# Summing a paged cache's four pieces per sample by accumulating gathers, three samples in turn, instead of by VectorE additions

## The reference, cut to what matters

```python
s16 = kv_cmp.reshape(B, n16, CMP_STRIDE, 2, KVH_D, HD_D).sum(axis=2)
cmp = (s16[:, :-1] + s16[:, 1:]) / CMP_BLOCK
kc = rms_norm(cmp[:, :, 0], kc_gain)
vc = cmp[:, :, 1]
```

## Time and profile before

| | |
|---|---|
| median of 3 runs | 1304.25 us (1300.81 to 1307.91) |
| the profiled execution, its own time | 1298.92 us |
| its span (first to last instruction) | 1297.1 us, so 1.8 us lie around it |
| mean granted TensorE clock | 0.979 |
| busy in the span: PE, DVE, POOL, ACT | 94%, 43%, 39%, 34% |

### The profile page before, as it was taken

One profiled execution on the slowest core, in us unless ns is written; L12 is line 12 of the kernel. 1 busy time (PEld: TensorE's weight loads), 2 busy tenths in 40 slices (PEclk: granted clock), 3 DMA queues, 4 the chain that ended last, 5 costly groups with the idle time before them and its releaser, 6 DMA issues.

```text
span 1297.1 us, 24311 instructions
## 1 busy us (share of the span) xinstructions
PE 1213.3 (94%) x10336; PEld 1137.1 (88%) x10336; DVE 557.2 (43%) x893; ACT 441.1 (34%) x713; POOL 503.7 (39%) x262
## 2 busy tenths in 40 slices
PE   7999979989999888899999878999999999999998
PEld 7998969988888877678887657999999999999998
DVE  4247643472337766664566554544322000222001
ACT  5432221124362223355444333333434211333111
POOL 3374441263135563322222451444343434344340
PEclk9999989889999999899999999999999999999999
DMA  5410101642136464311113493322222222222222
GB/s 202 148 65 34 66 33 58 140 127 66 51 99 212 163 210 131 130 57 58 65 51 129 159 337 116 139 98 83 97 84 94 87 93 98 81 97 81 99 81 82
DMA packets 47688, 139.52 MB, mean 108 GB/s; under 512 B 4470, under 2 KB 16090, under 8 KB 47210
## 3 DMA queue, kind: packets, MB, share of 16 engines
q1 hardware_dynamic: 37234, 100.50, 23.2%
q0 software_dynamic: 10368, 37.75, 8.5%
HBM read 129.98 MB, written 8.49 MB: 107 GB/s over the span
## 4 chain that ended last, share of the span: by engine, by line
PE 78%; DVE 13%; DMA 3%; issue 2%; ACT 2%; POOL 2%; SPq 0%; DVEq 0%; ACTq 0%
PE PS L614 46%; PE PS L847 11%; PE PS L659 7%; PE PS L715 2%; DVE M L1798 2%; PE PS L982 1%; DMA M<-cache_slc_kv,idx 1%; PE PS L1011 1%; PE PS L995 1%; DVE M L1801 1%; DMA M<-cache_cmp_kv,idx 1%; DVE xT L1662 1%; PE PS L810 1%; POOL WL L2198 1%; DVE M L1702 1%
## 5 line engine op out<-in xcount | busy, mean ns | idle before, releaser
L2198 POOL TENSOR_TENSOR WL<-M,WH 128x1024 fp32r<-128x1024 f32 x159 | 389.0, 2450 | 694.0 <-ACT WH L1189 693.7
L1189 ACT CAST WH<-M 128x1024 fp32r<-128x1024 f32 x159 | 165.8, 1046 | 266.3 <-DMA M<-weights 266.2
L614 PE MATMUL PS<-hH,WH 128*128 128x260 f32 x1040 | 215.5, 289 | 4.7 <-DVE M L1630 3.6
L614 PE MATMUL PS<-hH,WL 128*128 128x260 f32 x1040 | 212.7, 287 | 0.0
L614 PE MATMUL PS<-hL,WH 128*128 128x260 f32 x1040 | 212.3, 286 | 0.0
L614 PEld LDWEIGHTS PS<-hH,WH 128*128 128x128 f32 x1040 | 164.3, 193 | 8.2 <-issue 7.8
L614 PEld LDWEIGHTS PS<-hL,WH 128*128 128x128 f32 x1040 | 163.6, 192 | 0.0
L614 PEld LDWEIGHTS PS<-hH,WL 128*128 128x128 f32 x1040 | 163.5, 192 | 0.0
L847 PE MATMUL PS<-hH,WH 128*128 128x260 f32 x384 | 113.3, 295 | 4.5 <-ACT tmp L1345 2.9
L847 PE MATMUL PS<-hL,WH 128*128 128x260 f32 x384 | 109.7, 286 | 0.0
L847 PE MATMUL PS<-hH,WL 128*128 128x260 f32 x384 | 109.4, 285 | 0.0
(11 more groups left out here) (383 smaller groups left out, 2220.4 us busy)
## 6 DMA issues: line engine op xcount, KB each, us to landing
M<-weights SPq DMA_DIRECT2D x159, 512.0 KB, 3.3
M<-cache_win_kv POOLq DMA_DIRECT2D x7, 512.0 KB, 5.2
spill<-xT SPq DMA_DIRECT2D x1, 2080.0 KB, 8.7
M<-spill SPq DMA_DIRECT2D x1, 2080.0 KB, 7.8
M<-x_prompt SPq DMA_DIRECT2D x4, 512.0 KB, 5.4
con<-tables SPq DMA_DIRECT2D x1, 1437.5 KB, 12.5
M<-state_gla SPq DMA_DIRECT2D x2, 512.0 KB, 6.5
M<-state_hgrn SPq DMA_DIRECT2D x2, 512.0 KB, 11.0
```

Of the source, the lines that this page charges most:

```text
L614: last = mm(PS[:, bank + h, 0:HALF], w[:, slot_of(n), k, :], x[:, HALF * h:HALF * h + HALF], start=(start and k == k0 and w is WH and x is ...
L1189: nc.scalar.copy(WH[:, at].rearrange("p k n -> p (k n)"), WR[:, at]).then_inc(sem("w_hi"), 1)
L2198: p.tensor_tensor(WL[:, at].rearrange("p k n -> p (k n)"), WR[:, at], WH[:, at].rearrange("p k n -> p (k n)"), ALU.subtract).then_inc(sem( ...
```

## The change

The pieces of a sample are no longer brought to three slots in turn and added by DVE. A sample has one slot: its first piece is gathered into it, and the other three are gathered with an addition (`compute_op=ALU.add`), so that the DMA adds what it reads from the cache to what stands in the slot. A piece may be gathered only when the one before it in that slot has landed, so POOL waits for that slot's semaphore (`xc0` to `xc2`) ahead of each accumulating gather. Three samples go in turn, each in a slot of its own: samples 0 to 2, then 3 to 5, then 6 and 7 (numbered in the order in which they are taken). There are 32 gathers as before.

DVE is left with one L1798-like addition (512 columns) and the fold to 256 per sample. A table says at which step: C_GATHER for POOL, C_FOLD for DVE, C_PRODUCT for PE, C_COPY for DVE's copies out of bank 5. The third running sum takes the space of the former partial sum. The cache pieces after the stage wait for 8 in place of 32 counts of `c_free`.

```diff
-        CPIECES = [(x, c) for x in CSAMPLES for c in range(4)]
-        CSUM, CPART = [zt[:, 4, T:T + 512], zk[:, 1536:2048]], zk[:, 512:1024]
+        C_GATHER = {k: (n, c) for a, b, at in ((0, 3, -1), (3, 6, 15), (6, 8, 30)) for c in range(4)
+                    for n in range(a, b) for k in [at + 3 * c + n - a]}
+        C_FOLD = {12: 0, 13: 1, 14: 2, 28: 3, 29: 4, 30: 5, 42: 6, 43: 7}
+        C_PRODUCT = {15: (0, 1), 18: (2,), 31: (3,), 34: (4, 5), 45: (6, 7)}
+        C_COPY = {16: 0, 32: 2, 35: 4, 46: 6}
+        CSUM = [zt[:, 4, T:T + 512], zk[:, 1536:2048], zk[:, 512:1024]]
...
-                if k % 6 == 2 and 8 <= k <= 50:
-                    compressed_sum((k - 8) // 6)
+                for c in C_PRODUCT.get(k, ()):
+                    compressed_sum(c)
...
-                if k % 3 == 1 and k < 48:
-                    for q in (2 * (k // 3), 2 * (k // 3) + 1):
-                        n, c = q // 4, q % 4
-                        total = CSUM[n % 2]
-                        w = CRING[q % 3]
-                        dve.wait_ge(sem(f"xc{q % 3}"), 16 * (q // 3 + 1))
-                        if c == 0 and n >= 2:
-                            dve.wait_ge(sem("c_mm"), n - 1)
-                        v.tensor_tensor(CPART if c else total, w[:, 0:512], w[:, 512:1024], ALU.add).then_inc(sem("c_free"), 1)
-                        dve.wait_ge(sem("c_free"), q + 1)
-                        if c:
-                            step(v.tensor_tensor(total, total, CPART, ALU.add))
-                        if c == 3:
-                            v.tensor_tensor(total[:, 0:256], total[:, 0:256], total[:, 256:512], ALU.add)\
-                                .then_inc(sem("c_fold"), 1)
+                if k in C_FOLD:
+                    n = C_FOLD[k]
+                    w, total = CRING[n % 3], CSUM[n % 3]
+                    dve.wait_ge(sem(f"xc{n % 3}"), 64 * (n // 3 + 1))
+                    if n >= 3:
+                        dve.wait_ge(sem("c_mm"), n - 2)
+                    v.tensor_tensor(total, w[:, 0:512], w[:, 512:1024], ALU.add).then_inc(sem("c_free"), 1)
+                    dve.wait_ge(sem("c_free"), n + 1)
+                    v.tensor_tensor(total[:, 0:256], total[:, 0:256], total[:, 256:512], ALU.add)\
+                        .then_inc(sem("c_fold"), 1)
...
+            def compressed_gather(n, c):
+
+                if n >= 3 and c == 0:
+                    gp.wait_ge(sem("c_free"), n - 2)
+                if c:
+                    gp.wait_ge(sem(f"xc{n % 3}"), 16 * (4 * (n // 3) + c))
+                at = NI + NS * c + CSAMPLES[n]
+                src, row = rows("cache_cmp_kv"), bass.IndirectOffsetOnAxis(idx[:, at:at + 1], 0)
+                if c:
+                    gp.indirect_dma_start(CRING[n % 3], None, src, row, compute_op=ALU.add).then_inc(sem(f"xc{n % 3}"), 16)
+                else:
+                    gp.indirect_dma_start(CRING[n % 3], None, src, row).then_inc(sem(f"xc{n % 3}"), 16)
```

More of the change, by code:

```diff
@@ L858, in compressed_sum @@
                     pe.wait_ge(sem("sh_ev"), n // 2)
-                mm(PS[0:NCMP, 5, 256 * (x % 2):256 * (x % 2) + 256], C("shift", 0, NCMP), CSUM[n % 2][:, 0:256],
+                mm(PS[0:NCMP, 5, 256 * (x % 2):256 * (x % 2) + 256], C("shift", 0, NCMP), CSUM[n % 3][:, 0:256],
                    start=True, stop=True).then_inc(sem("c_mm"), 1)
@@ L1789, in mix_step @@
                             .then_inc(sem("mix_add"), 1)
[L1790 to L1806 removed]
+                if k in C_FOLD:
[8 more added lines that the diff above has]
+                        .then_inc(sem("c_fold"), 1)
+                if k in C_COPY:
+                    n = C_COPY[k]
                     x = CSAMPLES[n]
@@ L2262, in _ @@
             rows = lambda name: A[name].rearrange("o n (r t) a k d -> (o n r) (t a k d)", t=4)
-            def compressed_gather(q):
-                if q >= 3:
-                    gp.wait_ge(sem("c_free"), q - 2)
-                x, c = CPIECES[q]
-                gp.indirect_dma_start(CRING[q % 3], None, rows("cache_cmp_kv"),
-                                      bass.IndirectOffsetOnAxis(idx[:, NI + NS * c + x:NI + NS * c + x + 1], 0))\
-                  .then_inc(sem(f"xc{q % 3}"), 16)
+            def compressed_gather(n, c):
[9 more added lines that the diff above has]
+                    gp.indirect_dma_start(CRING[n % 3], None, src, row).then_inc(sem(f"xc{n % 3}"), 16)
             def mix_step(k):
@@ L2278, in mix_step @@
                     lower(N_MIX + 12 * bi + 3 * m + 1 + (s + 1) // 2)
-                if k % 3 == 2 and k < 47:
-                    for q in (2 * (k // 3) + 3, 2 * (k // 3) + 4):
-                        if q < len(CPIECES):
-                            compressed_gather(q)
+                if k >= 2 and k in C_GATHER:
+                    compressed_gather(*C_GATHER[k])
             def cache_piece(n):
@@ L2288, in cache_piece @@
                 if n == 0:
-                    gp.wait_ge(sem("c_free"), len(CPIECES))
+                    gp.wait_ge(sem("c_free"), NS)
                 if n == 2:
@@ L2310, in _ @@
             gp.wait_ge(sem("prod"), units_to_free(N_MIX - 4))
-            compressed_gather(0)
-            compressed_gather(1)
-            compressed_gather(2)
+            for n in range(3):
+                compressed_gather(n, 0)
             lower(N_MIX)
```

2 lines of the change are left out of this document (removed).

## The result

| | before | after |
|---|---|---|
| median of 9 runs | 1307.23 us | 1292.12 us |
| lowest and highest | 1300.76, 1314.66 | 1290.76, 1300.18 |
| the profiled execution | 1298.92 us | 1290.87 us |
| its mean granted clock | 0.979 | 0.979 |

The ratio after to before is 0.990, with a 95% interval of 0.9873 to 0.9927: 13 us faster. The forecast was 1288 us and a ratio of 0.9875. Between the two profiled executions the difference is 8.05 us where the forecast had 16.4. So two things have to be explained: why the traces show half of what was forecast, and why the medians show more than the traces. One further execution of the kernel before, among those timed beside the experiment one_later2, took 2333 us and is left out of all ratios.

The account below looks back on a forecast made before the run. PE sets the time, its idle stretches hanging on DVE's sums. Ceiling 19.2 + 5.5 = 24.7 us, less 5.6 new waits and 2.7 clock, gives 16.4, say 16: 1304.25 - 16 = 1288 us, range 1283 to 1313.

Parts of the forecast that it names:

- What bounds the kernel: 382 to 549 us: PE sets the time; nearly all its 24.65 us idle end on DVE, directly or through ACT.
- the 19.2 us named: PE's idle time put down to DVE's sums: waits for gating, `bL`, L2026, L1405 and the tanh, to be removed.
- the five waits that I called the largest: PE's waits in 382 to 549 us: five make 21.0 of 24.65 us idle, none on a lower part.
- What is removed: DVE's additions and folds, 56.7 us busy, 9.1 us waiting for pieces; ceiling of gain 24.7 us with the clock.
- L: Time from issue to landing of an accumulating gather: 6.6 us taken, lower bound 5.1, upper bound 10.2.
- The new waits: PE's waits behind landings, lower parts and folds: 2.5 at steps 12 to 15, 2.1 at 28 to 31, 1.0 at 42 and 43.
- no change: Rival: L of 8.5 to 10.5 us, new waits sum to 21 us at 10.2, 1303 us; chance 0.12.
- The clock: PE's lower clock level up to 549 us costs 5.5 us; half, 2.7 us, was left in.
- The slower one: Rival: landing chain holds POOL and PE, L beyond 10.5 us; about 1335 us at L = 15; chance 0.18.
- That the gain is given back: Rival: PE waits for weight chunks and lower parts instead, leaving 3 to 5 us gain, 1300 us; chance 0.06.
- the signs named for being right: Additions under 15 us, gating and `bL` waits few us, gaps at steps 4 and 12 closed, landing 6 to 7 us.
- the signs for being wrong: Landings over 10 us with POOL and PE waiting, or DVE idle over 10 us before L1800; would turn the sign.

Follow-up runs that it names:

- one_later2: later2 with only each sample's first piece gathered, so the sums lack three pieces; 1275.48 us, 0.9744 of the kernel before.
- later2: Changed kernel with tables moved: folds at steps 16 to 18, 34 to 36, 47, 48, later gather rounds started later; sums complete; 1276.54 us, 0.9759 of before.
- solo: Changed kernel in which only the first slot's samples (0, 3, 6) get their three accumulating gathers, the others only the first piece; 1289.3 us.
- plain: Changed kernel with each sample's three later gathers overwriting the slot instead of adding, all waits kept; 1283.67 us, 0.9815 of before.
- one_piece: Changed kernel with only each sample's first piece gathered, the other 24 gathers left out, folds kept; 1284.07 us, 0.9827 of before.
- later: Changed kernel with tables moved: folds at steps 16 to 18, 32, 34, 35, 46, 47, later gather rounds three steps later; sums complete; 1283.81 us, 0.9823 of before.
- narrow: Kernel before with DVE's first and running additions (L1798, L1801) cut from 512 to 16 columns, gathers and waits unchanged; 1293.22 us, 0.9886 of before.
- bef_b: Kernel before, unchanged, executed and profiled once more to see where its slower executions lose time; 1308.24 us.

## Why the prediction was right, and what in it was not

**What bounds the kernel** was read rightly. PE's idle time hung on DVE's sums, and 18.5 of the 19.2 us named are to be had: later2 has them. That the changed kernel has only 6.8 of them is a matter of the new waits. One reading was loose: the five waits that I called the largest leave out one of 2.7 us in 8 places, on L1788; the sum is 21.6 and not 21.0, and still without a lower part.

**What is removed** was right line by line: the waits for `bL`, for L2026, for L1405 and for the tanh went as named. The additions came to 14.6 us, just under the 15 given, though the prediction's own 1.1 us a sample would have made 9.

**The mis-sized term is L, the landing of an accumulating gather**: 6.6 us in the prediction, 8.8 measured. The 6.6 is right for one gather alone (6.5 in solo). The step that failed is the one from one transfer to three: I worked out the engine time of a transfer, 1.53 + 1.5 us, laid it on the latency, and did not multiply it by the three samples in turn, which gives 8.4 us (with the 2.79 measured) before any weight is moved. The DMA share of 0.50 that I held against a crowd was the mean of the stretch before; in 455:478 it was 0.65 already. The Trainium skill, Collectives: The Full Stack, part 3, says that a reducing step has two source reads and so runs at half the rate of a copying one. The trace agrees on the engine time, 2.79 against 1.53 us, a factor of 1.8. The Trainium skill's fit in DMA: Bandwidth & Descriptors, Anatomy of one DMA, is low for these gathers: with a second read it gives an estimate of 4.4 us, against 6.5 measured for one alone.

**The new waits** followed. With 2.5 + 2.1 + 1.0 = 5.6 us forecast, after has 13.2: 2.35 for the lower part behind a gather that POOL issued late, at 415.77 us, 1.27 and 0.98 behind the folds of steps 12 and 13 (forecast for this round 2.5, measured 4.6 together), 1.67 and 6.88 in the second round (forecast 2.1, measured 8.6), and hardly anything at 42 and 43 (forecast 1.0). By the prediction's own working, 5.6 us at 6.6 and 21 at 10.2, an L of 8.8 gives 15. It had set the bound between forecast and no change at 8.5, so on L alone the case fell just past it, and the two traces say the same: 19.2 - 13.2 = 6.0 us of idle time gained (6.8 measured in the stretch), and nothing from the clock.

**Unforeseen: the fold beside the lower part.** I took 0.69 us for each of the eight additions, though the earlier trace rows had one of 2.87 us. In the new order the additions of steps 12, 13, 28 and 42 run beside POOL's lower parts and take 1.00, 1.89, 3.75 and 1.84 us. This is 3.1 of the 6.88 us in after, and most of what plain and one_piece still wait for. The Trainium skill, SBUF — State Buffer, Who interferes with whom, says that a DVE instruction with two SBUF inputs contends with a GpSimd instruction that reads SBUF. The traces agree and give the size. An addition that begins during a lower part ends a fixed time after that part's end, however long it has stood: 0.54 to 0.57 us for 512 columns in before, after, plain, one_piece and later, and 0.02 to 0.05 us for the 16 columns of narrow. So it stands until POOL is done and then does its work. Additions with no lower part beside them take 0.68 or 0.69 us, and so do the seven in before, plain, one_piece and later that began up to 0.45 us ahead of a part; one of plain, which began 0.41 us ahead of two parts, took 5.67, and why that one stood is open. This was at work in the kernel before, too, and more than I read in the earlier trace rows: eight of its 56 additions ran beside a lower part and took 1.66 to 2.9 us, some 14 us more than at 0.69 each, and each of its four gaps of PE of over 2 us comes behind one of them. How much of its 24.65 us of idle time such standing made, no run separates.

**The clock.** I put the low clock of before at 5.5 us and expected half of it back. That sum ran to 549 us, and part of its low clock lies behind the start of step 48: in 543.55:549 the clock is 0.52, where after has 1.00 in 537.25:545, so this part was gained. Within the stretch, at 0.97, the prediction's working gives an estimate of 0.06 x 163.28 x 0.41 = 4.0 us for before. later2, at a clock of 0.99, has PE busy for 135.74 us, 2.9 less than before and 4.1 less than after. So in the stretch after gets nothing back and loses 1.2 us more. Its low clock lies in two places. In 405:428 it is 0.85, where before has 1.00: one run of 72 matmuls from 407.96 on takes 10.39 us instead of 8.87 without a gap ahead of it, and the 36 behind the gap of 2.35 us take 6.10 instead of some 4.6. Behind the gap of 6.88 us it is 0.50 in 479:483. The first run of 72 is no matter of the landings: one_later2, with no accumulating gather at all, has one of 10.39 us at the same steps.

**Why the medians are further apart than the traces.** The prediction laid the difference of one execution on the median, as if both kernels spread alike. The trace of before is of an execution near the lowest of its kind; that of after is too, but after's nine runs have their median only 1.3 us above it, before's 8.3 us. bef_b shows what the middle of before looks like: 8 us more of clock in the stretch. After, at 1292.12, lies 15.1 us under before's 1307.23, 13 by the ratio. That this comes so near to the 16 us forecast is luck in good part: it comes from two misses with opposite signs, new waits of 13.2 instead of 5.6 us and a low clock in before that its trace did not show in full. Trace against trace, the gain was 8.05 us for 16.4. Why before's clock varies more in this stretch from run to run was not settled; narrow, the same program with shorter additions, stays within 1290.0 to 1295.8.

**The rivals.** The slower one needed L over 10.5 us and is out. That the gain is given back, by waits for lower parts, was given 0.06 and half of its mechanism came: 4.4 us of waits for L2197, behind gathers of 1.55 us and weight chunks that land late in full DMA engines, not from a faster PE; in plain, with gathers of 0.96 us and weight chunks that land in 4.4 and 6.0 us in the two windows, 0.4 us are left. Of the signs named for being right, the landing (8.8 us for 6 to 7), the gap at step 12 (1.27 us are left of 3.92), the waits on the gating (8.2 us again) and the 16 us at the start of step 48 (6.3) did not come. One of the signs for being wrong did, DVE idle for over 10 us before L1800 (12.3), and it did not turn the sign.

## What to carry to other kernels

An accumulating DMA takes work from an engine, but here it asked the DMA engines for 1.8 times the time per byte: price a chain of them by all the transfers in flight together, and set the consumer behind that, not behind the latency of one. Before placing a short instruction with two SBUF inputs, look at what POOL does at that time, and at how soon another engine needs what stands behind it; where the folds stand was worth as much here (9 us) as the landings (8 us). A mean duration can hide this: look at the median and the longest as well. And where the executions of a kernel lie 15 us apart, look at a second trace before laying the difference of two traces on the medians.

## What the hardware showed unexpectedly

- An accumulating indirect gather of 512 KB (128 rows of 4 KB) holds POOL for 1.55 us against 0.96, also at half the size; it lands in 6.5 us alone, 7.6 with two and 8.8 with three in turn, and in 5.8 at half the size with three in turn. A plain one lands in 5.1 to 5.4.
- It takes 1.26 us more of all 16 DMA engines than the 1.53 of a plain one, and no less when it is alone (some 3.1 us in all in solo).
- A DVE addition that began during a lower part of POOL stood until POOL was done: it ended 0.54 to 0.57 us after it at 512 columns, 0.02 to 0.05 us after it at 16. Beside two parts in a row this made 3.75 us (after) and 5.67 us (plain) of 0.69.
- An addition of 16 columns takes 0.18 us in the median when nothing holds it, and up to 2.34 us beside a lower part, nearly as long as one of 512 columns (2.87).
- In the kernel before, the same matmuls in the same stretch took 138.63, 143.13 or 146.95 us from execution to execution, with the same idle time of PE, at clocks of 0.97, 0.94 and 0.91.
